# Modulation products two at a time inside the attentions of a two-layer diffusion step

## Chip, cores and metric

One core of a Trainium2 chip runs the whole program. The metric is the device time of one execution in microseconds (us); less is better.

## The reference

Two trunk layers over 384 tokens: 128 context tokens and 256 latent tokens, D = 1024. What matters here, for each layer `l`:

```
sh1, sc1, g1, sh2, sc2, g2 = split(silu(c) @ w_ada[l] + b_ada[l], 6)   # adaLN, c and c_ctx; w_ada[l] is 1024 x 6144
h  = rmsnorm(x, norm1_g[l]) * (1 + sc1) + sh1
qa, ka, va, ub, qc, kc, vc = split(h @ w_in[l])
oA = differential attention(qa, ka, va)       # 4 heads, two maps each: softmax 0 - lam * softmax 1
oB = multi-scale pooling(ub)
oC = windowed attention(qc, kc, vc, sink)     # 8 heads, keys within 128, a sink
x  = x + g1 * (sum_n sigmoid(h @ w_gate[n]) * (o_n @ w_branch[n])) @ w_out[l]
h2 = rmsnorm(x, norm2_g[l]) * (1 + sc2) + sh2
x  = x + g2 * channel_mixer(h2)               # SwiGLU in layer 0, top-2-of-8 experts in layer 1
```

All inputs are float32. The new keys and values of the context tokens are outputs too.

## The kernel before

Tokens lie in three blocks of 128. Every engine has its own instruction order, written out by hand, and the engines meet at semaphores. Big weight matrices come through a ring of three slots in SBUF (`raw`, 1 MB each, two DMAs of 512 KB from SyncE's queue, function `halves`, L498). Most slots are split into a high part (`whi`, ScalarE) and a low part (`wlo`, VectorE), and multiplied in three passes (L734 to L736).

**The modulation products.** `w_ada` of a layer is 24 slots of 256 columns. A product (`ada_product`, L751) is eight small matmuls, 128 rows by 32 columns each, of the conditioning vectors against one raw slot of float32; it needs no split. All the products of one phase add into PSUM bank 7. Its last matmul raises `mm_done`, and SyncE starts the load of the slot three further on in the order only when that semaphore says that this slot's user is done. Phases 2 to 5 are the four attentions (layer 0: differential, windowed; layer 1: the same), with 8, 7, 6 and 6 products. The first two of each (numbers 0 and 1) run together before step 0; the others stand in the steps that `ADA_STEPS` (L80) names. Behind the products of a phase come, in the same ring, the two gate slots and the branch slot of the projection after the attention.

**An attention** (`attention`, kind 0 differential, kind 1 windowed) has twelve steps t: four heads or head pairs by three blocks of queries. Where t is a multiple of three the queries are context tokens with 128 keys, otherwise there are 384 keys. In step t TensorE runs, in this order,

- `scores(t + 2)`, for t from 2 to 9 (L977); it waits for the exponentials of step t, whose banks it reuses
- the modulation products of this step
- `transposes(t)` of the weights (L995); it waits for VectorE's `normal(t)`
- `values(t - 1)` (L1011); it waits for ScalarE's copy of the transposed weights

ScalarE runs in step t `exps(t + 1)` (L1662), which waits for VectorE's maxima of t + 1 and for `transposes(t - 1)`, and then the copy of the transposed weights (`pt_copy`, L1673). VectorE runs, for t from 3 on, `maxima(t)` (L2153; in kind 1 with a mask before it, L2151) and then `normal(t - 1)` (L2161 to L2164, or L2166 to L2168). In kind 0 it also copies a head's output after step 5, 8 and 11 (L2183), and in kind 1 it adds up a branch merge after `normal(4)` (`merge_sum`, L2208, which is queued ahead of `maxima(6)`). Near the end ScalarE splits the first gate slot in two halves (`gate_hi`, L1498). After step 11 TensorE goes on with the gate projection (L1068 and after).

S, P, T and V stand below for the scores, product, transposes and values of a numbered step or product: T9 is `transposes(9)`, P4 the product with i = 4. M is maxima, E exponentials, N `normal`.

Of the kernel before, what the change touches and what calls it, by code (L numbers as in the profile page):

```python
# [76 lines left out]
EARLY_BUF = {0: 0, 1: 1, 2: 2, 3: 3, 4: 4, 5: 0, 7: 1, 9: 2}  # L77
EARLY = 5
GROUPS = ADA_SLOTS[0] // 2
ADA_STEPS = {2: (1, 3, 5, 7, 9, 10), 3: (1, 4, 6, 8, 10), 4: (1, 4, 6, 9), 5: (1, 4, 6, 9)}  # L80
assert all(2 + len(ADA_STEPS[p]) == ADA_SLOTS[p] <= 16 for p in ADA_STEPS)
SQS = (0, 1, 1 + N_HALF, 2 + N_HALF)
SQ0 = (0, BLK, BLK + 5 * N_HALF, BLK + 5 + 5 * N_HALF)
# [56 lines left out]
def prefix_step_kernel(nc, a, outs, const):  # L140
    y_prompt, y_sample, new_dk, new_dv, new_wk, new_wv = outs
    ctx = ExitStack()
    with ctx:
# [239 lines left out]
        def ada_slot(phase, i):  # L383

            if phase == 0:
                return FIRST_ADA[i]
            if phase == 1:
                return ADA_SLOTS[0] + 3 + RING * i
            l, kind = (phase - 2) // 2, (phase - 2) % 2
            return gate_slot(l, kind + 1, 0, 0) - ADA_SLOTS[phase] + i  # L390
# [17 lines left out]
        def ada_raw(n):  # L408

            return early[:, EARLY_BUF[n], :] if n in EARLY_BUF else raw[:, n % RING, :]  # L410
# [43 lines left out]
        def weight_col(t):  # L454

            return 1 + (T - P if t % 3 == 0 and t else 0)
# [20 lines left out]
        def raw_wait(eng, n, more=0):  # L477
            if n in EARLY_BUF:
                eng.wait_ge(side_in[EARLY_BUF[n]], early_wait(n))
            else:  # L480
                eng.wait_ge(raw_in[n % RING], more + 32 * raw_turn(n))
# [249 lines left out]
        def _(pe):  # L731
# [10 lines left out]
            def ada_product(phase, i):  # L742

                n, last, bank = ada_slot(phase, i), ADA_SLOTS[phase] - 1, 7
                if phase == 0:
                    i, last = i % 2, 1
                raw_wait(pe, n)
                w = ada_raw(n).rearrange("p (k c) -> p k c", k=KD)
                for k in range(KD):
                    j = k % 4  # L750
                    mm = pe.matmul(ps[32 * j:32 * j + 32, bank, 0:256], sil32[:, k, 30 - 2 * i:62 - 2 * i], w[:, k, :],  # L751
                                   start=(i == 0 and k < 4), stop=(i == last and k >= 4), tile_position=(0, 32 * j))
                mm.then_inc(mm_done, 1)
# [17 lines left out]
            def ada_end(phase, g=0):  # L771
                n = 2 * (GAP_SLOTS[phase] if phase in GAP_SLOTS else ADA_SLOTS[phase]) if phase else 4
                pe.wait_ge(ada_row, ada_turn(phase) if phase else g + 1)
                for c in range(2):
                    mm = pe.matmul(ps[:, 7, 256 + 32 * c:256 + 32 * c + n], adarow[:, c * P:(c + 1) * P], pick[:, 0:n],
                                   start=True, stop=True)
                mm.then_inc(ada_turned, 1)
# [188 lines left out]
            def scores(l, kind, t):  # L966

                h, qb = t // 3, t % 3
                if t >= 2:
                    pe.wait_ge(e_done, 24 * l + 12 * kind + t - 1)  # L970
                nk, k0 = (P, 0) if qb == 0 else (T, P)
                q, kk = (qTA, kTA[:, h, k0:k0 + nk]) if kind == 0 else (qTC, kTC[:, h // 2, k0:k0 + nk])
                for m in range(2):
                    r = slice(64 * m, 64 * m + 64)
                    c0 = score_col(t) if kind else 0
                    out, lhs = ps[:, 2 * (t % 2) + m, c0:c0 + nk], q[r, h, qb * P:(qb + 1) * P]
                    mm = pe.matmul(out, lhs, kk[r], start=True, stop=True)  # L977
                mm.then_inc(s_done, 1)

            def attention(l, kind):  # L980

                st0 = 24 * l + 12 * kind
                it0 = 24 * l + 12 * kind
                phase = 2 + 2 * l + kind

                def transposes(t):
                    pe.wait_ge(p_done, st0 + t + 1)
                    if kind:
                        pe.wait_ge(pt_evac, it0 + t)
                    elif it0 + t >= 2:  # L990
                        pe.wait_ge(pt_evac, it0 + max(t - 1, 0))
                    k0 = kind * weight_col(t)
                    for m in range(1 + kind):
                        for kb in range(1 if t % 3 == 0 else 3):
                            mm = pe.transpose(ps[:, 4 + (m if kind else t % 2), kb * P:(kb + 1) * P],  # L995
                                              ebuf[:, t % 2, m, k0 + kb * P:k0 + (kb + 1) * P], ident)
                    mm.then_inc(tp_done, 1)

                def values(t):
                    h, qb = t // 3, t % 3  # L1000
                    pe.wait_ge(pt_evac, it0 + t + 1)
                    grp = 8 * l + 4 * kind + h
                    if qb == 0 and grp >= 1:
                        pe.wait_ge(o_evac, grp)
                    c = slice(h * P, (h + 1) * P) if kind == 0 else slice(512 + (h // 2) * 64, 576 + (h // 2) * 64)
                    keys = [vtok[:, 0, c]] if qb == 0 else [vtok[:, 1, c], vtok[:, 2, c], ctxv[:, c]]
                    for kb, v in enumerate(keys):
                        k = slice(kb * P, (kb + 1) * P)
                        for m in range(1 + kind):
                            rows, x = (slice(64 * m, 64 * m + 64), ptm[:, t % 2, m, k]) if kind else (slice(0, P), pt[:, t % 2, k])  # L1010
                            mm = pe.matmul(ps[rows, 6, qb * P:(qb + 1) * P], v, x, start=(kb == 0),  # L1011
                                           stop=(kb == len(keys) - 1))
                    mm.then_inc(pv_done, 1)

                scores(l, kind, 2)
                scores(l, kind, 3)
                pe.wait_ge(merge_top, 2 * l + kind + 1)
                ada_product(phase, 0)
                ada_product(phase, 1)
                if kind == 0:  # L1020
                    pe.wait_ge(merge_done, 6 * l + 2)
                else:
                    pe.wait_ge(merge_read, 4 * l + 2)
                for t in range(12):
                    if t >= 2 and t + 2 < 12:
                        scores(l, kind, t + 2)
                    if t in ADA_STEPS[phase]:
                        ada_product(phase, 2 + ADA_STEPS[phase].index(t))
                    transposes(t)
                    if t >= 1:  # L1030
                        values(t - 1)
                    if t == 11 and kind == 1:
                        ada_end(phase)
                values(11)
# [422 lines left out]
            for l in range(DEPTH):  # L1457
                if l:
                    mean_squares(2 * l)
                input_projection(l)  # L1460
                branch(l, 0)
                attention(l, 0)
                branch(l, 1)
                attention(l, 1)
                branch(l, 2)
                out_projection(l)
                mean_squares(2 * l + 1)
                if l == 0:
                    units()
                else:  # L1470
                    router()
                    experts()
# [1196 lines left out]
```

## Time and profile before

| | |
|---|---|
| median of three runs | 1483.82 us (1482.88 to 1486.86) |
| profiled execution, own time | 1485.04 us |
| its span, first to last instruction | 1482.8 us |
| TensorE busy | 1454.4 us, 98% of the span |
| VectorE, ScalarE busy | 901.8 us (61%), 734.1 us (50%) |
| mean granted share of TensorE's clock | 0.996 |

The span is what the trace shows; the own time has 2.24 us around it. The four attentions begin with their products 0 and 1 at 194.83, 276.27, 844.07 and 924.18 us, and the next gate projection starts at 220.56, 307.29, 868.48 and 954.33 us.

### The profile page before, as it was taken

The page shows a single profiled execution, that of the slowest core. Times are in us where ns is not written, and L with a number is a line of the kernel's source. Part 1 is how long each engine was busy: PE and PEld are TensorE (multiplying, and loading weights), DVE is VectorE, ACT ScalarE, POOL GpSimd, SP SyncE. Part 2 cuts the span into 40 slices and gives each one's busy share as a digit, 9 for nine tenths or more (in the row PEclk, how much of TensorE's full clock was granted, in tenths as well). Part 3 has the DMA queues.
Part 4 walks back from the last instruction along what each step waited for, and adds up shares of the span by engine and source line. Part 5 has one row for each costly group of instructions (what it writes and reads, how often), then busy time and mean ns, then how long its engine had stood idle before and what let it go on. Part 6 is the DMA issues. An engine that isn't in the chain of part 4 may idle for free.

```text
span 1482.8 us, 22302 instructions
## 1 busy us (share of the span) xinstructions
PE 1454.4 (98%) x8911; PEld 1277.9 (86%) x8911; DVE 901.8 (61%) x1077; ACT 734.1 (50%) x872; POOL 49.4 (3%) x53
## 2 busy tenths in 40 slices
PE   7999999999999999999999999999899999999998
PEld 5788969789999999998889879699788888888884
DVE  4543265555654245336532373736799999999886
ACT  4433354453442242225434272733678787787753
POOL 0100000000000000001000000000000000000020
PEclk9999999999999999999999999999999999999999
DMA  9854365468763445364432371646499999999991
GB/s 328 285 174 150 114 222 176 137 203 272 240 186 102 129 125 142 114 213 145 152 125 91 102 234 59 225 144 206 141 378 385 383 390 389 383 383 388 350 336 50
DMA packets 228137, 324.36 MB, mean 219 GB/s; under 512 B 8373, under 2 KB 154718, under 8 KB 227790
## 3 DMA queue, kind: packets, MB, share of 16 engines
q1 hardware_dynamic: 219728, 296.02, 58.8%
q0 software_dynamic: 6256, 23.77, 4.4%
q10 hardware_dynamic: 2062, 3.24, 0.6%
q8 instruction: 71, 1.16, 0.3%
q14 instruction: 20, 0.16, 0.0%
HBM read 308.05 MB, written 14.95 MB: 218 GB/s over the span
## 4 chain that ended last, share of the span: by engine, by line
PE 93%; DVE 3%; SPq 2%; ACT 1%; DMA 1%; issue 1%; ACTq 0%; DVEq 0%
PE ps L734 26%; PE ps L736 26%; PE ps L735 26%; PE ps L751 2%; PE ps L977 2%; PE ps L1011 1%; PE ps L995 1%; SPq L498 1%; PE ps L1233 1%; PE ps L1273 1%; DMA early<-in_w_ada_dram 1%; PE ps L832 1%; PE ps L761 0%; PE ps L956 0%; ACT ebuf L1662 0%
## 5 line engine op out<-in xcount | busy, mean ns | idle before, releaser
L734 PE MATMUL ps<-hhi,whi 128*128 128x384 f32 x824 | 276.6, 336 | 0.3 <-DVE hidlo L2554 0.3
L736 PE MATMUL ps<-hhi,wlo 128*128 128x384 f32 x824 | 275.4, 334 | 0.0
L735 PE MATMUL ps<-hlo,whi 128*128 128x384 f32 x824 | 275.3, 334 | 0.0
L1980 DVE TENSOR_TENSOR wlo<-raw,whi 128x2048 fp32r<-128x2048 f32 x64 | 146.4, 2289 | 176.5 <-ACT whi L1488 164.6
L734 PEld LDWEIGHTS ps<-hhi,whi 128*128 128x128 f32 x824 | 154.7, 188 | 2.4 <-issue 2.0
L735 PEld LDWEIGHTS ps<-hlo,whi 128*128 128x128 f32 x824 | 154.7, 188 | 0.3
L736 PEld LDWEIGHTS ps<-hhi,wlo 128*128 128x128 f32 x824 | 154.6, 188 | 0.0
L2440 DVE TENSOR_TENSOR wlo<-mraw,whi 128x2048 fp32r<-128x2048 f32 (+2 forms) x72 | 143.5, 1992 | 15.0 <-ACT whi L1759 14.6
L1759 ACT ACTIVATE whi<-mraw 128x2048 fp32r<-128x2048 f32 (+2 forms) x72 | 120.9, 1679 | 58.5 <-PE ps L736 57.4
L1488 ACT ACTIVATE whi<-raw 128x2048 fp32r<-128x2048 f32 x60 | 114.5, 1911 | 70.4 <-PE ps L736 58.8
L2440 DVE TENSOR_TENSOR wlo<-raw,whi 128x2048 fp32r<-128x2048 f32 (+2 forms) x72 | 144.2, 2018 | 8.1 <-ACT whi L1759 7.7
L734 PE MATMUL ps<-whi,xgh 128*128 128x512 f32 (+1 forms) x384 | 145.9, 380 | 0.2 <-DVE xgl L2429 0.2
L736 PE MATMUL ps<-whi,xgl 128*128 128x512 f32 (+1 forms) x384 | 142.7, 372 | 0.0
L735 PE MATMUL ps<-wlo,xgh 128*128 128x512 f32 (+1 forms) x384 | 142.7, 372 | 0.0
L1759 ACT ACTIVATE whi<-raw 128x2048 fp32r<-128x2048 f32 (+2 forms) x72 | 121.6, 1698 | 30.9 <-PE ps L736 30.7
L734 PE MATMUL ps<-whi,hhi 128*128 128x512 f32 (+1 forms) x285 | 108.6, 381 | 2.8 <-issue 2.0
L2540 DVE TENSOR_TENSOR wlo<-raw,whi 128x2048 fp32r<-128x2048 f32 (+1 forms) x36 | 76.1, 2113 | 57.9 <-ACT whi L1736 57.9
L736 PE MATMUL ps<-whi,hlo 128*128 128x512 f32 (+1 forms) x285 | 106.1, 372 | 0.0
L735 PE MATMUL ps<-wlo,hhi 128*128 128x512 f32 (+1 forms) x285 | 105.9, 372 | 0.0
L1736 ACT ACTIVATE whi<-raw 128x2048 fp32r<-128x2048 f32 (+1 forms) x36 | 63.8, 1771 | 54.4 <-PE ps L736 54.4
L734 PEld LDWEIGHTS ps<-whi,xgh 128*128 128x128 f32 x384 | 72.1, 188 | 12.2 <-issue 2.0
L736 PEld LDWEIGHTS ps<-whi,xgl 128*128 128x128 f32 x384 | 72.1, 188 | 10.2
(397 smaller groups left out, 2495.0 us busy)
## 6 DMA issues: line engine op xcount, KB each, us to landing
raw<-in_w_ada_dram SPq DMA_DIRECT2D x62, 512.0 KB, 5.2
raw<-in_w_gate_dram SPq DMA_DIRECT2D x48, 512.0 KB, 4.6
raw<-in_w_ex_up_dram SPq DMA_DIRECT2D x24, 1024.0 KB, 7.8
raw<-in_w_ex_down_dram SPq DMA_DIRECT2D x24, 1024.0 KB, 7.8
raw<-in_w_in_dram SPq DMA_DIRECT2D x43, 512.0 KB, 6.1
raw<-in_w_ex_gate_dram SPq DMA_DIRECT2D x16, 1024.0 KB
mraw<-in_w_ex_gate_dram SPq DMA_DIRECT2D x16, 1024.0 KB, 8.4
mraw<-in_w_ex_down_dram SPq DMA_DIRECT2D x16, 1024.0 KB, 8.6
```

Of the source, the lines that this page charges most:

```text
L498: sp.dma_start(dst[i], src[i]).then_inc(side_in[EARLY_BUF[n]] if n in EARLY_BUF else raw_in[n % RING], 16)
L734: pe.matmul(out, s[0], m[0], start=first, stop=False, **kw)
L735: pe.matmul(out, s[0], m[1], start=False, stop=False, **kw)
L736: return pe.matmul(out, s[1], m[0], start=False, stop=last, **kw)
L751: mm = pe.matmul(ps[32 * j:32 * j + 32, bank, 0:256], sil32[:, k, 30 - 2 * i:62 - 2 * i], w[:, k, :], start=(i == 0 and k < 4), stop=(i == ...
L977: mm = pe.matmul(out, lhs, kk[r], start=True, stop=True)
L1488: act.activation(whi[:, n % RING, :], raw[:, n % RING, :], copy).then_inc(hi_done, 1)
L1736: act.activation(whi[:, s % RING, 0:used], raw[:, s % RING, 0:used], copy).then_inc(hi_done, 1)
L1759: act.activation(whi[:, m % RING, c:E_USED[m]], mraw[m % MRAW][:, c:E_USED[m]], copy).then_inc(hi_done, 1)
L1980: dve.tensor_tensor(wlo[:, n % RING, :], raw[:, n % RING, :], whi[:, n % RING, :].bitcast(F32), ALU.subtract).then_inc(lo_done, 1)
L2440: dve.tensor_tensor(wlo[:, m % RING, c:E_USED[m]], mraw[m % MRAW][:, c:E_USED[m]], whi[:, m % RING, c:E_USED[m]].bitcast(F32), ALU.subtrac ...
L2540: dve.tensor_tensor(wlo[:, s % RING, 0:used], raw[:, s % RING, 0:used], whi[:, s % RING, 0:used].bitcast(F32), ALU.subtract).then_inc(lo_d ...
```

## The change

The same products run in the same order, with the same weights and into the same bank. Only the steps in which they stand are others: where one product stood in each of four to six steps, two now stand in each of two or three steps (the second attention keeps a single one in step 10). In the loop the single test becomes a loop over all products of the step.

```diff
--- before.py
+++ after.py
@@ -77,7 +77,7 @@
 EARLY_BUF = {0: 0, 1: 1, 2: 2, 3: 3, 4: 4, 5: 0, 7: 1, 9: 2}
 EARLY = 5
 GROUPS = ADA_SLOTS[0] // 2
-ADA_STEPS = {2: (1, 3, 5, 7, 9, 10), 3: (1, 4, 6, 8, 10), 4: (1, 4, 6, 9), 5: (1, 4, 6, 9)}
+ADA_STEPS = {2: (3, 3, 6, 6, 9, 9), 3: (3, 3, 7, 7, 10), 4: (4, 4, 9, 9), 5: (4, 4, 9, 9)}
 assert all(2 + len(ADA_STEPS[p]) == ADA_SLOTS[p] <= 16 for p in ADA_STEPS)
 SQS = (0, 1, 1 + N_HALF, 2 + N_HALF)
 SQ0 = (0, BLK, BLK + 5 * N_HALF, BLK + 5 + 5 * N_HALF)
@@ -1024,8 +1024,9 @@
                 for t in range(12):
                     if t >= 2 and t + 2 < 12:
                         scores(l, kind, t + 2)
-                    if t in ADA_STEPS[phase]:
-                        ada_product(phase, 2 + ADA_STEPS[phase].index(t))
+                    for i, step in enumerate(ADA_STEPS[phase]):
+                        if step == t:
+                            ada_product(phase, 2 + i)
                     transposes(t)
                     if t >= 1:
                         values(t - 1)
```

`ADA_STEPS[phase][i]` is the step of product i + 2. The first attention goes from P2 to P7 in steps 1, 3, 5, 7, 9, 10 to 3, 3, 6, 6, 9, 9; the second from P2 to P6 in 1, 4, 6, 8, 10 to 3, 3, 7, 7, 10; the third and fourth from P2 to P5 in 1, 4, 6, 9 to 4, 4, 9, 9.

## Rows read from the trace of the kernel before

**Rows 1.** The page's busy time, share of the span and instructions of each engine:

```profile
PE 1454.4 (98%) x8911; PEld 1277.9 (86%) x8911; DVE 901.8 (61%) x1077; ACT 734.1 (50%) x872; POOL 49.4 (3%) x53
```

**Rows 2.** The page's chain that ended last, shares of the span by engine:

```profile
PE 93%; DVE 3%; SPq 2%; ACT 1%; DMA 1%; issue 1%; ACTq 0%; DVEq 0%
```

**Rows 3.** Stretches (us): busy PE, PEld, DVE, ACT, POOL (instructions), clock, DMA share, GB/s:

```profile
197.00:221.00 24.00, 23.48 (x215) 14.89 (x215) 16.71 (x43) 17.20 (x55) 0.00 (x0) 1.00 1.00 321
276.00:308.00 32.00, 30.49 (x326) 18.57 (x323) 21.14 (x51) 21.72 (x59) 0.00 (x0) 1.00 0.73 231
843.00:869.00 26.00, 25.02 (x224) 15.93 (x224) 19.81 (x47) 17.43 (x55) 0.00 (x0) 1.00 0.77 243
924.00:955.00 31.00, 29.42 (x308) 18.02 (x307) 21.87 (x51) 21.99 (x61) 0.00 (x0) 1.00 0.63 204
```

**Rows 4.** TensorE's timeline, first attention's opening: start, us, what [idle before]:

```profile
194.83 1.93 PE L751 MATMUL ps<-raw,sil 128*32 128x256 f32 x32
196.69 0.33 PE L995 MATMUL ps<-cst,ebuf 128*128 128x128 f32 x1
196.95 1.07 PE L751 MATMUL ps<-raw,sil 128*32 128x256 f32 x16
197.95 0.55 PE L995 MATMUL ps<-cst,ebuf 128*128 128x128 f32 x3
...
198.65 0.92 PE L977 MATMUL ps<-kTA,qTA 64*128 64x384 f32 x4
199.62 0.55 PE L995 MATMUL ps<-cst,ebuf 128*128 128x128 f32 x3
```

**Rows 5.** VectorE's timeline there: the weights of step 2 finished:

```profile
198.94 0.62 DVE L2164 SCALAR_TENSOR_TENSOR ebuf<-ebuf,small 128x384 f32<-128x384 f32 x1
```

**Rows 6.** TensorE's timeline, first attention's closing:

```profile
215.49 0.33 PE L995 MATMUL ps<-cst,ebuf 128*128 128x128 f32 x1
...
218.42 0.55 PE L995 MATMUL ps<-cst,ebuf 128*128 128x128 f32 x3 [0.23 <-DVE ebuf L2164]
...
219.87 0.71 PE L1011 MATMUL ps<-pt,vtok 128*128 128x128 f32 x4 [0.24 <-ACT pt L1673]
```

**Rows 7.** Timeline of all engines, from scores of step 8 to weights of step 7:

```profile
207.74 0.92 PE L977 MATMUL ps<-kTA,qTA 64*128 64x384 f32 x4
...
208.70 0.96 DVE L2153 TENSOR_REDUCE small<-ps 128x2 f32<-128x768 f32 x1 [1.32 <-PE ps L977]
...
209.51 0.49 PE L977 MATMUL ps<-kTA,qTA 64*128 64x128 f32 x4
...
210.02 0.62 DVE L2164 SCALAR_TENSOR_TENSOR ebuf<-ebuf,small 128x384 f32<-128x384 f32 x1
```

**Rows 8.** TensorE's timeline, second attention:

```profile
281.53 0.88 PE L995 MATMUL ps<-cst,ebuf 128*128 128x128 f32 x6
...
289.31 0.87 PE L995 MATMUL ps<-cst,ebuf 128*128 128x128 f32 x6 [0.62 <-DVE ebuf L2168]
...
290.91 0.92 PE L977 MATMUL ps<-kTC,qTC 64*128 64x384 f32 x4
```

**Rows 9.** VectorE's timeline, second attention:

```profile
280.69 0.42 DVE L2168 TENSOR_SCALAR ebuf<-ebuf,small 128x384 f32<-128x384 f32 x1
...
286.31 1.75 DVE L2208 TENSOR_TENSOR macc<-macc,gbuf 128x1536 f32<-128x1536 f32 x1
...
293.75 0.41 DVE L2168 TENSOR_SCALAR ebuf<-ebuf,small 128x384 f32<-128x384 f32 x1
```

**Rows 10.** First attention's loads issued at 198.4 and at 202.7 us: time to landing:

```profile
DMA to landing us min/median/max: 7.6/8.2/8.7
...
DMA to landing us min/median/max: 6.3/6.9/7.4
```

**Rows 11.** The stretch with the lower clock, columns as in Rows 3:

```profile
678.40:685.20 6.80, 6.80 (x45) 4.61 (x48) 1.56 (x5) 0.26 (x1) 0.00 (x0) 0.50 0.48 157
```

**Rows 12.** TensorE's timeline there, a product between other stages:

```profile
680.49 1.93 PE L761 MATMUL ps<-gap,sil 128*32 128x256 f32 x16
```

## The prediction

> **What bounds the kernel now.** I read the page's busy times and its chain of waits first. TensorE is busy 98% of the span and holds 93% of the chain [rows 1, 2]: a microsecond that is added to or taken from its own queue arrives at the end, unless a wait takes it up. Then the busy time by stretch: in the four attentions TensorE is still busy for 23.5 of 24.0, 30.5 of 32.0, 25.0 of 26.0 and 29.4 of 31.0 us, 4.6 us of idling in all, while VectorE and ScalarE work 66 to 76% of each [rows 3]. So these stretches are TensorE's work with a few small waits, and the question is which waits the products now cover. The timelines say that step by step.
>
> **What a product costs.** Alone it takes 1.00 us from its start to the next instruction (196.95 to 197.95). The pair ahead of step 0 takes 1.86 (194.83 to 196.69) [rows 4]. So the second of a pair costs 0.86, and each pair saves 0.14 against two single ones. The change makes 3 + 2 + 2 + 2 = 9 new pairs: 9 x 0.14 = 1.26 us less work. It adds no instruction and no DMA.
>
> The Trainium skill (TensorEngine Tiling (Array Packing), Key Properties) has a rule for this: changing the tiling mode, not just the tile, drains the engine. By that rule each pair makes two mode changes fewer; the pair in the trace agrees in sign, and the page gives no time.
>
> **What limits TensorE when no product stands in a step.** Three chains, read from starts and ends.
> - Kind 0, middle: S8 starts at 207.74, M8 at 208.70, and N7, behind it on VectorE, ends at 210.02 + 0.62 = 210.64 [rows 7]. So T(t+1) can't start before S(t+2) + 2.95 (0.05 for the semaphore). TensorE's own work between them is S8 with T6 and V5 (207.74 to 209.51, 1.77 [rows 7]) and S9, of one block of keys (0.43, its 0.49 less the overlap). With a product among them there is no wait; without one T7 must wait.
> - Kind 1, the same with the mask: S8 starts at 290.91 [rows 8], N7 ends at 293.75 + 0.41 = 294.16 [rows 9]: S + 3.30.
> - Both ends of an attention. Opening: E2 waits for T0, and N2 ends at 198.94 + 0.62 = 199.56 [rows 5], which is when T2 starts (199.62) [rows 4]. Closing in kind 0: E11 follows T9 on ScalarE and N11 follows E11, so T11 starts 218.42 - 215.49 = 2.93 after T9 [rows 6] whatever TensorE does between.
>
> **First attention.** P2 leaves step 1. There it was covered: without it, V0 and S4 wait for ScalarE and T2 starts at 199.62 as before. In step 3, beside P3, it costs its 0.86. P4 and P5 go from steps 5 and 7 together into step 6: -0.14, and by the chain counts about 0.06 of wait each in T5 and T8, +0.12. P7 leaves step 10, where it stood inside the fixed 2.93 between T9 and T11; in step 9, ahead of T9, it costs 0.86. Last, V11 waited until 219.87 [rows 6] for a ScalarE copy behind half a gate split; from T11 to the projection it was 220.56 - 218.42 = 2.14, and with that wait gone T11, V10 and V11 take about 1.8: -0.3 to -0.36. Sum 0.86 - 0.14 + 0.12 + 0.86 - 0.36 = **+1.3**.
>
> **Second attention.** T2 followed S4 at 281.53 without a wait [rows 8], while N2 had ended at 280.69 + 0.42 = 281.11 [rows 9]: taking P2 out of step 1 gives back 0.37, no more. P2 and P3 in step 3 cost 1.86 and P3 leaves step 4 (-1.00), but T5 had a wait of 0.62 there [rows 8], for VectorE, behind `merge_sum` (286.31, 1.75 us [rows 9]), that swallows most of it. Counting E5 behind T3 and the output copy on ScalarE, T5 comes out 0.12 later than before. Then P4 leaves step 6 and P5 step 8 (-2.00, and a wait of 0.19 before S10 goes), and the pair in step 7 costs 1.86: -0.33. Sum **-0.2**. P6 stays in step 10.
>
> **Third attention.** P2 from covered step 1 into step 4: +0.86. P4 leaves step 6: -1.00, but S8 to T7 is then 1.77 + 0.43 = 2.20 of work against 2.95: T7 waits 0.75, and V6 and T8 wait 0.2 more behind it: +0.94. P4 in step 9 beside P5: +0.86. Sum **+1.66**.
>
> **Fourth attention.** T2 -0.37; P2 into step 4 +0.86; the wait before T5 (0.69 here) goes; P4 leaves step 6 -1.00; T7 waits 0.84 (S + 3.30 against 2.46 of work); two waits before S10 and T8 (0.32) go; P4 in step 9 +0.86. Sum -0.37 + 0.86 - 0.69 - 1.00 + 0.84 - 0.32 + 0.86 = **+0.2**.
>
> Together 1.33 - 0.20 + 1.66 + 0.18 = **+3.0 us**. The 1.26 saved is in it: without it the waits would add 4.2.
>
> **The loads.** A product also frees a slot. In the first attention the load of slot 5 starts after P2, at 202.75 where it was 198.4, and P5 wants it at 209.4, so 6.2 us are left for its second half. At 202.7 us a load with two others in flight took 6.3 to 7.4 us [rows 10]; now only one is in flight, its own 1 MB takes 3 us at the 321 GB/s of this stretch [rows 3], and it lands at about 207.6. I cost it at nothing; 1.8 us cover it. Slot 7 starts after P4 (209.5) for 216.2, with the same margin. In the third and fourth attention gate slot 1 now loads after P4 in step 9, some 6 us later; ScalarE splits it about 8 us after that issue, against landing times of 3.5 to 8.7. In the worst of these only ScalarE would wait, with 2.5 us before TensorE needs the slot. What follows an attention depends on it alone (the projections are relative to TensorE's progress), so I carry the sum to the end in full.
>
> The profiled execution's span of 1482.8 would become 1485.8 and its own time 1488.0. It lay 1.2 above the median; on the median 1483.82 + 3.0 = **1486.8 us**.
>
> **Rivals.**
> 1. *The loads decide; slower.* If slot 5 and slot 7 take the 8.7 us of the worst row [rows 10], P5 waits from 209.4 to 211.9 and P7 2.4 more; 3.0 + 4.9 gives 1491.7. For it: the memory queue is full in this stretch. Against: that row stood behind two other loads. It decides from landing times over 6.2 us. 10%.
> 2. *The pairing pays; not slower, or a little faster.* The waits are small and ScalarE and VectorE are a quarter to a third idle [rows 3]. If they catch up while TensorE is in a pair, only the 0.14 per pair is left: 1483.8 - 1.3 = 1482.6, -0.1%. Against: catching up is bounded, since S(t+2) must have run before VectorE can go ahead, and it is issued before the pair. It decides from T7 in the third attention: does it wait? 17%.
> 3. *The clock; slower.* In the attentions TensorE had its 2.4 GHz throughout, gaps of up to 0.7 us included (granted clock 1.00 [rows 3]). But it fell to 1.2 GHz for 6.8 us at 678.4 [rows 11], when the engine had just run the sums of squares, matmuls of a single column; a product took 1.93 there [rows 12] against 1.07 [rows 4]. Such a stretch costs up to 3.4 us. The change thins out TensorE's work in the opening and in steps 5 to 7, and it shifts all later stages by some us; if one more such stretch appears, 3.0 + 3.4 gives 1490.2. It decides from a granted clock under 1.00 in any of the four stretches, or a third dip elsewhere. 6%. The Trainium skill (TensorE: Matmul & The Clock Gate, Part 1) has the rule that activity holds the clock up and lack of it lets it drop; the trace agrees with that at 678 us, and shows it in no attention.
>
> **Numbers.** Forecast 64%, rival 2 17%, rival 1 10%, rival 3 6%, something else 3%. My counts could be wrong by 1.5 us in either direction, the difference between medians by about as much (the three runs spread over 4 us). About 0.3%, 4.5 us, is what a measurement of this kernel tells from no change, so the forecast and rival 2 both mean "no change" nearly always. Same 0.83, slower 0.15, faster 0.02. The range takes in rival 2 and reaches almost to rival 3, and leaves out rival 1: 1482.6 to 1490.
>
> **What the changed profile would show.** Pairs of 1.86 us everywhere. T2 at 199.6 in the first attention with about 0.8 us of waits before S4 and V0; T11 there with a wait near 1.0 instead of 0.23; T7 of the third and fourth attention waiting 0.75 and 0.84 for VectorE. The attentions, from product 0 to the gate projection, longer by 1.3, -0.2, 1.7 and 0.2 us (25.7, 31.0, 24.4 and 30.2 before). Idling in the four stretches about 4.2 us more. No product waiting for a load. The prediction is wrong if a product does wait for one, if T2 of the first attention moves with P2, or if the shift is not found again at the end of the span.

## The result, and the profile after

The changed kernel takes 1487.23 us in the median of 11 runs (1485.74 to 1489.99) against 1483.82 in 11 runs of the kernel before (1482.48 to 1487.17). The two medians are 3.4 us apart; the ratio over all runs is 1.0018, 95% interval 1.0010 to 1.0026: 2.7 us more, between 1.5 and 3.9. That is a loss that eleven runs can tell from nothing, and inside the 0.3% that counted as "no change". The forecast was 1486.8, +3.0.

The busy times of the page are those of before [rows 1] to within 0.2%. The instructions are the same, and so are their kinds:

```profile
span 1485.1 us, 22302 instructions
...
PE 1452.3 (98%) x8911; PEld 1277.8 (86%) x8911; DVE 902.1 (61%) x1077; ACT 733.2 (49%) x872; POOL 49.4 (3%) x53
```

The four attentions, each timed in the timeline from its product 0 to the first matmul of the gate projection behind it:

| attention | before | after | difference | predicted |
|---|---|---|---|---|
| first | 25.74 | 27.72 | +1.98 | +1.33 |
| second | 31.02 | 30.81 | -0.20 | -0.20 |
| third | 24.40 | 26.05 | +1.65 | +1.66 |
| fourth | 30.15 | 30.23 | +0.08 | +0.18 |
| sum | | | +3.51 | +2.97 |

The predicted values are from the sums of the prediction. The two stretches right behind a differential attention, up to the windowed one, are the same to 0.02 us in both traces (55.71 and 55.70 before, 55.71 and 55.69 after). The profiled spans differ by 2.3 us, not 3.5; where the other 1.2 went is told below.

TensorE's timeline of the changed kernel, first attention. To be read beside [rows 4] and [rows 6], 0.11 us earlier at its start:

```profile
194.72 1.93 PE L751 MATMUL ps<-raw,sil 128*32 128x256 f32 x32
...
198.40 0.92 PE L977 MATMUL ps<-kTA,qTA 64*128 64x384 f32 x4 [0.64 <-ACT ebuf L1663]
199.51 0.55 PE L995 MATMUL ps<-cst,ebuf 128*128 128x128 f32 x3 [0.19 <-DVE ebuf L2165]
...
201.50 1.94 PE L751 MATMUL ps<-raw,sil 128*32 128x256 f32 x32
203.37 0.33 PE L995 MATMUL ps<-cst,ebuf 128*128 128x128 f32 x1
...
208.34 1.93 PE L751 MATMUL ps<-raw,sil 128*32 128x256 f32 x32
210.20 0.33 PE L995 MATMUL ps<-cst,ebuf 128*128 128x128 f32 x1
...
215.31 1.07 PE L751 MATMUL ps<-raw,sil 128*32 128x256 f32 x16
216.69 1.07 PE L751 MATMUL ps<-raw,sil 128*32 128x256 f32 x16 [0.30 <-DMA raw<-in_w_ada_dram]
217.69 0.33 PE L995 MATMUL ps<-cst,ebuf 128*128 128x128 f32 x1
...
219.43 0.46 PE L1011 MATMUL ps<-pt,vtok 128*128 128x128 f32 x2 [0.42 <-DVE oraw L2184]
220.62 0.55 PE L995 MATMUL ps<-cst,ebuf 128*128 128x128 f32 x3 [0.73 <-DVE ebuf L2165]
```

The pairs take 1.87 us (201.50 to 203.37) and 1.86. T2 starts 4.79 us after product 0, in both kernels, now with waits of 0.64 before S4 and 0.19 before T2 in the place of the product of step 1. T11 waits 0.73 where it waited 0.23, and V9 0.42 before it. And one thing was not forecast: the second product in step 9 waits 0.30 for its load (216.69), so those two take 2.38. Two other kernels with the same steps from 6 on don't have that wait; more on it below.

The same view of the third and the fourth attention, where T7 waits for VectorE, 0.69 and 0.79 where 0.75 and 0.84 were forecast:

```profile
859.75 0.49 PE L977 MATMUL ps<-kTA,qTA 64*128 64x128 f32 x4
860.94 0.55 PE L995 MATMUL ps<-cst,ebuf 128*128 128x128 f32 x3 [0.69 <-DVE ebuf L2165]
```

```profile
943.47 0.49 PE L977 MATMUL ps<-kTC,qTC 64*128 64x128 f32 x4
944.76 0.87 PE L995 MATMUL ps<-cst,ebuf 128*128 128x128 f32 x6 [0.79 <-DVE ebuf L2169]
```

Busy time by stretch, columns as in [rows 3]. The first stretch had 0.5 us of idling before; it has 2.4 now, the third 2.2 where it had 1.0. Taken from product 0 to the gate projection, the four attentions idle for 8.7 us where they idled for 4.6, that is 4.1 more for the 4.2 of the prediction:

```profile
197.00:221.00 24.00, 21.61 (x199) 13.12 (x197) 16.64 (x42) 15.36 (x52) 0.00 (x0) 1.00 0.92 307
...
843.00:869.00 26.00, 23.81 (x213) 14.84 (x211) 19.06 (x46) 14.98 (x52) 0.00 (x0) 1.00 0.59 186
```

### The profile page after: what moved, and what is told of

Same layout as the page of the kernel before. It is cut to its first block, busy times and chain, and to the rows that moved or that the text cites. A ratio compares the mean times of both kernels' runs of the same rounds, so it can differ in the third digit from the quotient of the medians.

```text
span 1485.1 us, 22302 instructions
## 1 busy us (share of the span) xinstructions
PE 1452.3 (98%) x8911; PEld 1277.8 (86%) x8911; DVE 902.1 (61%) x1077; ACT 733.2 (49%) x872; POOL 49.4 (3%) x53
## 4 chain that ended last, share of the span: by engine, by line
PE 92%; DVE 3%; DMA 2%; ACT 1%; issue 1%; SPq 0%; DVEq 0%; ACTq 0%
PE ps L734 26%; PE ps L736 25%; PE ps L735 25%; PE ps L751 2%; PE ps L977 2%; PE ps L1011 1%; PE ps L995 1%; DMA mraw<-in_w_ex_up_dram 1%; PE ps L761 1%; DMA early<-in_w_ada_dram 1%; PE ps L832 1%; PE ps L1274 1%; DVE macc L2001 0%; PE ps L956 0%; DVE wlo L2441 0%
```

## The experiments

Two theories. **Cover**: a product costs nothing where TensorE would wait for the softmax chain anyway, 1.00 us alone or 0.86 behind another elsewhere, and the change moves products out of covered steps. **Pairs**: two at a time cost by themselves, by the burst that holds up ScalarE and VectorE or by the loads that start later. The table has what each kernel's own trace shows for the four attentions, as differences to the kernel before; the two rows of the thin kernels are read below. Each row is one traced execution. The changed kernel was also timed over eleven runs, by_waits and mixed over twelve each; of the others there is only the one time (1483.9 to 1491.3 us), and nothing is concluded from it.

| kernel | steps of the products | 1st | 2nd | 3rd | 4th |
|---|---|---|---|---|---|
| changed | 3,3,6,6,9,9 / 3,3,7,7,10 / 4,4,9,9 / 4,4,9,9 | +1.98 | -0.20 | +1.65 | +0.08 |
| thin_before | as before, four thin products | 0.00 | 0.00 | -0.07 | -0.45 |
| thin_after | as changed, the same four thin | +1.03 | -0.63 | +1.20 | -0.37 |
| open_back | 1,3,6,6,9,9 / 1,3,7,7,10 / 1,4,9,9 / 1,4,9,9 | +0.60 | -0.33 | +0.79 | +0.28 |
| late_back | 3,3,6,6,9,10 / 3,3,6,8,10 / 4,4,6,9 / 4,4,6,9 | +1.21 | +0.13 | +0.86 | -0.19 |
| pairs_covered | 1,3,5,7,10,10 / 1,4,4,7,10 / 1,4,10,10 / 1,4,10,10 | -0.10 | -1.03 | +0.11 | +0.10 |
| by_waits | 1,4,7,10,10,11 / 1,4,4,7,10 / 1,4,7,10 / 4,4,7,10 | +2.11 | -0.26 | -0.45 | -0.52 |
| loads_triple | 3,3,5,6,9,9 / 3,3,7,7,9 / 1,10,10,10 / 4,4,7,9 | +1.62 | -0.19 | +3.70 | -0.53 |
| halves | as before, each product cut in two | +1.29 | +0.44 | +1.09 | +0.33 |
| mixed | 1,3,5,7,10,10 / 1,4,4,7,10 / 1,4,7,10 / 4,4,7,10 | -0.14 | -0.59 | -0.45 | -0.53 |

All but the thin kernels and halves differ from the changed kernel only in the tuple `ADA_STEPS`.

### Thin products: the same work taken out of both kernels

Four products, one in each attention, keep only the last of their eight matmuls; what the other seven would have added is missing from the outputs. The edit, cut to its core:

```diff
-            def ada_product(phase, i):
+            def ada_product(phase, i, ks=range(KD)):
...
-                for k in range(KD):
+                for k in ks:
...
+                        thin = (phase, i) in ((2, 2), (3, 3), (4, 4), (5, 4))
+                        ada_product(phase, i, range(7, 8) if thin else range(KD))
```

> The kernel before, with four products cut to the last of their eight matmuls (so four column groups of the modulations are wrong by the parts left out): P2 (step 1) of the first attention, P3 (step 4) of the second, P4 (step 6) of the third, P4 (step 6) of the fourth. About 0.75 us of TensorE's work is gone in each. Cover theory (a product between the scores and the transposes of those steps stands where TensorE would wait anyway): the four attentions change by 0.0, 0.0, -0.06 and -0.5 us. Rival (TensorE's queue is the bound throughout, so products cost their time wherever they stand): -0.75 in each.

> The changed kernel with the same four products cut to their last matmul. Cover theory: here each of them stands on the path, so against the changed kernel the attentions shrink by 0.75, 0.5, 0.75 and 0.75 us (one that follows its pair's first may save 0.1 less). Rival (the change costs because of bursts or late loads, not by lost cover): the same savings as in the kernel before, whatever they are.

Measured, the saving is 0.00, 0.00, 0.07 and 0.45 us in the kernel before, and 0.96, 0.43, 0.45 and 0.45 in the changed one. TensorE's timeline of thin_before, first attention:

```profile
194.50 1.93 PE L751 MATMUL ps<-raw,sil 128*32 128x256 f32 x32
...
196.63 0.62 PE L751 MATMUL ps<-raw,sil 128*32 128x256 f32 x2
197.18 0.55 PE L996 MATMUL ps<-cst,ebuf 128*128 128x128 f32 x3
...
198.19 0.92 PE L978 MATMUL ps<-kTA,qTA 64*128 64x384 f32 x4 [0.24 <-ACT ebuf L1665]
199.30 0.55 PE L996 MATMUL ps<-cst,ebuf 128*128 128x128 f32 x3 [0.19 <-DVE ebuf L2167]
```

One matmul of the eight still takes 0.55 us to the next instruction (196.63 to 197.18), where the product took 1.00. So 0.45 us is what was really taken out, not 0.75: my size was off. That 0.45 goes into waits in the first attention (0.24 before S4, 0.19 before T2), and T2 starts 4.80 us after product 0, as before. In the first three attentions the product was covered. In the fourth it was covered in part: T7 now waits 0.24 for VectorE, but the waits behind it (0.19 before S10, 0.14 before T8) are gone, and the sum is 0.45 again. In the changed kernel every one of the four gives its whole 0.45 back. The first gives 0.96, since P7 waits for no load in this kernel: its last pair takes 1.87 (214.77 to 216.64). The thin product doesn't explain that, as both the load of P7's slot and P7 itself come 0.45 sooner. The cover theory holds in seven of the eight values as told, with 0.45 in the place of 0.75, and in the eighth with the load added. Queue-bound throughout is refuted: three of four products cost nothing before.

### Opening and closing put back, one at a time

> The changed kernel with the first of the moved products back in step 1: steps 1,3,6,6,9,9 / 1,3,7,7,10 / 1,4,9,9 / 1,4,9,9. Cover theory, against the kernel before: +0.5, -0.3, +0.8, +0.4 us (the changed kernel has +2.0, -0.2, +1.65, +0.1). In the third attention half of the loss goes, since T2 starts when VectorE lets it; in the fourth it gets worse by 0.3, since there step 1 is covered only in part and the product in step 4 was covered by the wait behind the merge sum. Rival (bursts): each loses in proportion to its pairs, so the first attention keeps two thirds, the third and fourth one half.

> The changed kernel with its later pairs undone in part: steps 3,3,6,6,9,10 / 3,3,6,8,10 / 4,4,6,9 / 4,4,6,9. Cover theory, against the kernel before: +0.8, +0.1, +0.9, -0.2 us. In the first attention the whole of the last pair's cost is gone, the wait of the last product for its load as well. Rival (the late load is what the change costs in the first attention): only the 0.3 to 0.5 us of that wait comes back there, so it stays at +1.5 or more.

open_back came out as counted: +0.60, -0.33, +0.79 and +0.28 were measured for +0.5, -0.3, +0.8 and +0.4. Its last pair of the first attention, in step 9 like that of the changed kernel, takes 1.86 and waits for no load. The rival's proportional shares would be about +1.3, +0.8 and 0 in the first, third and fourth. The third can't tell the two apart; the first and the fourth go with cover. late_back came out as counted in three attentions and at +1.21 instead of +0.8 in the first. There the last product is back in step 10 and waits for no load. ScalarE's timeline shows what is late in its place:

```profile
219.06 0.49 ACT L1674 ACTIVATE pt<-ps 128x384 f32<-128x384 f32 x1 [0.74 <-PE ps L995]
219.71 1.06 ACT L1499 ACTIVATE whi<-raw 128x1024 fp32r<-128x1024 f32 x1 [0.16 <-DMA raw<-in_w_gate_dram]
220.67 0.47 ACT L1674 ACTIVATE pt<-ps 128x384 f32<-128x384 f32 x1
```

The split of the first gate slot waits 0.16 for its load, the copy of T11's weights is queued behind it, and V11 waits 0.51 for that copy where it waited 0.24 before [rows 6]. SyncE had needed 1.58 us to issue the half ahead of it, slot 7's second, against a median of 0.51. The first row is that issue, the second, from a view of the next microsecond, how long the two gate halves then took:

```profile
L498 SPq DMA_DIRECT2D raw<-in_w_ada_dram x1: 1577/1577/1577, 210.1 to 210.1; - x1
```

```profile
L498 SPq DMA_DIRECT2D raw<-in_w_gate_dram x2: 508/630/751, 211.7 to 212.3; - x2
...
DMA to landing us min/median/max: 6.3/6.8/7.4
```

So the gate slot was issued at 211.7, where it was 211.1 before and 210.4 in the changed kernel. That the slow issue alone made it late is not shown: in the changed kernel its second half was issued 1.1 us sooner after product 0 (at 211.0), took 8.5 us and landed as far behind product 0. Of the 0.4 above the forecast 0.3 is V11's longer wait. The other 0.1 stands before T8, which comes 0.95 us later than in the kernel before, in this kernel as in the changed one; +0.84 was counted. The late-load rival named the wrong load and expected +1.5 or more; it fails too.

### Pairs where TensorE waits, and products by the waits

> Pairs, but only in steps where the chains leave TensorE waiting: steps 1,3,5,7,10,10 / 1,4,4,7,10 / 1,4,10,10 / 1,4,10,10. Cover theory: against the kernel before -0.1, -1.0, +0.2, 0.0 us, so a pair costs nothing by itself. Rival (two products at a time are what costs): a loss of 0.5 to 1 us per pair in each attention.

Measured -0.10, -1.03, +0.11, +0.10: a pair costs nothing by itself. The second attention, with a pair in step 4 behind `merge_sum`'s wait, is a full microsecond shorter.

> Products put where TensorE waits: steps 1,4,7,10,10,11 / 1,4,4,7,10 / 1,4,7,10 / 4,4,7,10. Cover theory: against the kernel before -0.8, -1.0, -0.4, -0.6 us, together -2.9, so about 0.2% faster (ratio 0.998). Rival (pairs cost by themselves, or the waits come back elsewhere, at the gate projection or in the loads): no gain, or a loss like that of the changed kernel in the attentions that have a pair (first, second, fourth).

Ratio 1.0014 (1.0004 to 1.0024): slower. This one missed. The third and fourth attention give what was told (-0.45, -0.52), the second -0.26 in place of -1.0, the first +2.11 in place of -0.8, and the stretch behind it another 1.58. In the second, with the same steps as in pairs_covered, P4 waited for its load and the pair took 0.77 longer:

```profile
291.03 1.07 PE L751 MATMUL ps<-raw,sil 128*32 128x256 f32 x16 [0.56 <-DMA raw<-in_w_ada_dram]
```

ScalarE and TensorE in the first:

```profile
216.91 0.49 ACT L1674 ACTIVATE pt<-ps 128x384 f32<-128x384 f32 x1 [1.03 <-PE ps L995]
220.62 1.06 ACT L1499 ACTIVATE whi<-raw 128x1024 fp32r<-128x1024 f32 x1 [3.22 <-DMA raw<-in_w_gate_dram]
221.59 0.47 ACT L1674 ACTIVATE pt<-ps 128x384 f32<-128x384 f32 x1
```

```profile
222.11 0.71 PE L1011 MATMUL ps<-pt,vtok 128*128 128x128 f32 x4 [2.87 <-ACT pt L1674]
```

With P5 in step 10 the first gate slot's load starts after step 10, and ScalarE waits 3.22 us for it, with the copy for V11 queued behind. My count for this kernel had the products' own loads in it and left out the gate slot's. TensorE then stands still for 2.87 us, and the clock goes:

```profile
223.30:226.70 3.40, 3.40 (x14) 3.40 (x12) 2.03 (x1) 1.92 (x3) 0.00 (x0) 0.51 0.85 309
```

For 3.4 us the granted clock is 0.51, and matmuls of the gate projection that take 0.34 take 0.52. The stretch up to the windowed attention, 55.7 us in every other trace, takes 57.29 here. The four attentions make +0.88 and this 1.58: 2.5 us together, and the ratio says 2.1 (0.6 to 3.6).

### An earlier load, and three in a row

> Steps 3,3,5,6,9,9 / 3,3,7,7,9 / 1,10,10,10 / 4,4,7,9. First attention: P4 alone in step 5, so the slot of P7 is loaded some 2 us earlier than in the changed kernel: if P7's wait there was for its load, it is gone and the last pair takes 1.86 us instead of 2.38; the attention comes to +1.4 against the kernel before (changed kernel +2.0). If the wait stays, it was not the load. Third attention: three in a row in step 10: 1.00 + 0.86 + 0.86 = 2.72 us if each product after the first saves 0.14; 2.86 if only one of them does; the attention +1.0. Second -0.1, fourth -0.5.

```profile
206.49 1.07 PE L751 MATMUL ps<-raw,sil 128*32 128x256 f32 x16
207.49 0.55 PE L995 MATMUL ps<-cst,ebuf 128*128 128x128 f32 x3
...
215.60 1.93 PE L751 MATMUL ps<-raw,sil 128*32 128x256 f32 x32
217.47 0.33 PE L995 MATMUL ps<-cst,ebuf 128*128 128x128 f32 x1
```

With P4 in step 5 the last pair takes 1.87 us, as was told for a wait that is the load's. It proves less than it was meant to, because open_back and thin_after lose the wait too, without an earlier P4. The attention stands at +1.62 against +1.98; +1.4 was told.

```profile
864.00 2.80 PE L751 MATMUL ps<-raw,sil 128*32 128x256 f32 x48
866.73 0.55 PE L995 MATMUL ps<-cst,ebuf 128*128 128x128 f32 x3
...
871.69 0.81 PE L1011 MATMUL ps<-pt,vtok 128*128 128x128 f32 x4 [2.90 <-ACT pt L1674]
```

Three in a row take 2.73 us: each product behind another saves 0.14. The third attention as a whole missed, +3.70 for +1.0, in the same way as by_waits: P3 in step 10 holds back the first gate slot (TensorE waits 2.90 before V11), and 3.4 us at half the clock follow (57.05 for 55.70 behind it).

### What the 0.14 us are

In the loop, with `ks` as in the thin kernels and `mm_done` raised by the second half alone:

```diff
                     if t in ADA_STEPS[phase]:
-                        ada_product(phase, 2 + ADA_STEPS[phase].index(t))
+                        ada_product(phase, 2 + ADA_STEPS[phase].index(t), range(4))
                     transposes(t)
+                    if t in ADA_STEPS[phase]:
+                        ada_product(phase, 2 + ADA_STEPS[phase].index(t), range(4, KD))
```

> The kernel before with each product inside the steps cut in two halves of four matmuls, one before the transposes and one after them; no work is left out, but TensorE changes between kinds of matmul twice more per product. If the 0.14 us that a pair saves is the price of such a visit, each half takes about 0.57 us to the next instruction (0.43 + 0.14), a product 1.14 in all. The attentions grow by 0.3, 0.4, 0.3, 0.2 us where this is not covered. Rival (the 0.14 is no price of changing kinds but a start-up of the first product of a step, such as waiting for its slot's semaphore): the second half takes 0.43.

```profile
196.85 0.64 PE L751 MATMUL ps<-raw,sil 128*32 128x256 f32 x8
197.42 0.55 PE L996 MATMUL ps<-cst,ebuf 128*128 128x128 f32 x3
197.90 0.64 PE L751 MATMUL ps<-raw,sil 128*32 128x256 f32 x8
198.47 0.49 PE L1012 MATMUL ps<-pt,vtok 128*128 128x128 f32 x2
198.88 0.92 PE L978 MATMUL ps<-kTA,qTA 64*128 64x384 f32 x4
```

Each half takes 0.57 us (196.85 to 197.42, 197.90 to 198.47), 0.43 + 0.14, the second as much as the first. So 0.14 is a price of each visit and no start-up of the step; the rival fails. The sizes of the attentions missed: +1.29, +0.44, +1.09, +0.33 for +0.3, +0.4, +0.3, +0.2. The neighbours pay too: T1 takes 0.48 to the next start, where it takes 0.39 ahead of V0 [rows 4: 197.95, with V0 at 198.34], and V0 takes 0.41, where it took 0.31. That is 0.2 more per product than I counted: the added visit, between transposes and values, costs some 0.33 in all.

### The placement that the runs point to

> Steps 1,3,5,7,10,10 / 1,4,4,7,10 / 1,4,7,10 / 4,4,7,10: each attention has the placement that came out best so far without holding back a gate slot's load. Theory (a product costs nothing where TensorE waits, 0.86 to 1.00 us elsewhere, provided that no load of a later slot comes late by it): the attentions take -0.1, -1.0, -0.45, -0.5 us against the kernel before, together -2.1 us or a ratio of 0.9986, and ScalarE's first half of the first gate slot waits for no load. Rival (the gain of the second attention seen in one run, and of the fourth in two, does not survive as time of the whole, because it is given back between the attentions): ratio 1.000.

Ratio 0.9989, 95% interval 0.9980 to 0.9997: 1482.98 us in the median of 12 runs against 1485.17 of 17 runs of the kernel before on the same chip. It beats the kernel before by 0.11%, and, by the two ratios, the changed one by about 0.3%; the two were not run side by side. The attentions took -0.14, -0.59, -0.45 and -0.53, together -1.71, and the ratio gives -1.6 (-3.0 to -0.4). ScalarE's split of the first gate slot waits for no load in the first and third attention. In the second, P4 in step 4 waited for its load:

```profile
285.38 1.07 PE L751 MATMUL ps<-raw,sil 128*32 128x256 f32 x16
286.68 1.07 PE L751 MATMUL ps<-raw,sil 128*32 128x256 f32 x16 [0.23 <-DMA raw<-in_w_ada_dram]
287.68 0.88 PE L995 MATMUL ps<-cst,ebuf 128*128 128x128 f32 x6
```

so 0.44 of the microsecond that pairs_covered had gained there is missing, though the two kernels have the same steps in this attention. The wait parts the pair too: it takes 2.30 (285.38 to 287.68). In pairs_covered it takes 1.87:

```profile
285.60 1.93 PE L751 MATMUL ps<-raw,sil 128*32 128x256 f32 x32
```

In by_waits, the third kernel with these steps, it took 2.63. What differs is the landing of slot 4's second half: 10.0 us after product 0 in pairs_covered, 10.6 here and 10.9 in by_waits, with P4 ready for it at 10.3. When it was issued doesn't order them: 3.5, 3.9 and 3.4 us after product 0. Here SyncE had taken 1.73 us over the issue of slot 3's second half, and in pairs_covered 1.35 over that of slot 4's first. So the margin is 0.3 us, and the load's own time varies by more than that, with steps that are the same. The 62 issues of halves of `w_ada` in the trace of before take 0.37 to 1.79 us, at a median of 0.51, from one and the same line of code. Why one sometimes takes three times as long stays open, and so does why the landing times spread.

## Why the prediction was right

**The time and its sign.** Forecast +3.0, measured +2.7 (1.5 to 3.9). The likeliest case came in, not a rival: pairs save 0.14 each, and the waits uncovered cost more. That the number came so close is in part luck. In the profiled execution the attentions took 3.51 us more, 0.5 of it by a load that was forecast to cost nothing, and the rest of the execution gave 1.2 back. Of the three signs of being wrong that the prediction names, T2 did not move with P2. A product did wait for a load, in the profiled execution. And the shift is found at the end of the span only as 2.3 us.

**What a product costs.** Right: 1.00 alone, 0.86 behind another, also for the third of three. The count of 9 pairs held but for one, which the load split. The Trainium skill's rule that a change of tiling mode drains the engine (TensorEngine Tiling (Array Packing), Key Properties) fits what halves shows, two visits at the same price; that the 0.14 us are a drain is argued, not shown. The prediction's "two mode changes fewer" for each pair is too many where scores stand ahead, which is so in steps 2 to 9. The rows have scores as `64*128` and transposes as `128*128`, so the kind of matmul changes there with or without a product. In halves the visits between transposes and values, both `128*128`, are the ones for which the neighbours pay 0.2 more.

**What limits TensorE.** Right in all three chains: T2 4.79 us after product 0 in both kernels; T11 2.93 us after T9 before, 220.62 - 217.69 = 2.93 after; T7 2.96 us after S8 in the third attention (857.98 to 860.94) for 2.95, and 3.30 in the fourth (941.46 to 944.76). The thin products show the other half, that work in those places was free before.

**Attention by attention.** Second, third and fourth within 0.1 us. The first took +1.98 for +1.33, and 0.52 of the difference is the pair with P7: in this execution the loads' 0 was too little. I gave slot 7 what its own 1 MB takes once the queue is free. It was issued at 209.5 and 209.9, as foreseen, and its halves took 4.5 us and more:

```profile
L498 SPq DMA_DIRECT2D raw<-in_w_ada_dram x2: 367/438/508, 209.5 to 209.9; - x2
...
DMA to landing us min/median/max: 4.5/5.6/6.8
```

The second half took the 6.8 us and landed 0.05 us before P7 starts at 216.69. thin_after and open_back have the same steps from 6 on, and there P7's slot is issued just as long before the last pair (5.8 us), with the gate slot's load behind it as well, its first half half a microsecond later, its second at 1.7 us and not 1.1. Its halves take 4.1 and 5.1 us, and 4.2 and 5.2, and P7 waits for nothing. thin_after:

```profile
DMA to landing us min/median/max: 4.1/4.6/5.1
```

So the load behind alone did not make it late. What differs more is the load ahead, slot 6, whose second half was issued at 204.2 in the changed kernel and at 203.6 in thin_after. It took 9.6 us, until 213.8, well into slot 7's time, and 6.9 us, until 210.5:

```profile
DMA to landing us min/median/max: 9.6/9.6/9.6
```

```profile
DMA to landing us min/median/max: 6.9/6.9/6.9
```

That this pushed slot 7 back is argued, and why it took 9.6 us stays open. P7 waited 0.30, the pair took 0.52 longer, and with T9 later by that it all went to the end. Without it the first attention comes to +1.46, and open_back (+0.60, and 0.86 for its product in step 1) and thin_after (+1.03, and 0.45) give 1.46 and 1.48. So the placement leaves P7 a margin that one of three such traces used up, and the forecast's 0 holds in the other two. Slot 5's landing, the one that the prediction worried about most, was in time. Rival 1 was thus right in kind for one product in one execution, and in size for a tenth (0.5 of 4.9). The remaining 0.13 is small waits: before T8 they are 0.21 (0.07 at S10, 0.14 at T8) where 0.12 was counted for T5 and T8, and the end of the attention gives back 0.33 and not 0.36.

**The carry to the end.** I carried the sum in full. Up to the next attention that is right to 0.02 us. Over the long stretches it can't be read from one execution: the second to third attention took 536.32 us for 536.78, the end 527.84 for 528.49. The granted clock may be part of it. Before, it fell to 0.50 for 3.4 us behind the last out projection; after, it didn't there:

```profile
1040.20:1043.60 3.40, 3.40 (x18) 3.40 (x18) 0.41 (x2) 1.29 (x2) 0.00 (x0) 0.50 0.00 0
```

```profile
1042.00:1046.00 4.00, 3.84 (x35) 3.76 (x35) 1.32 (x3) 1.78 (x4) 0.00 (x0) 1.00 0.06 23
```

Of the eleven traces of this study, all eleven have such a dip near 680 us; six have one near 395, and six, not the same, one near 1040. They come and go between kernels that are identical there. The 4 to 5 us that runs of one kernel spread over fit with that, but no run here separates it.

**Rival 3** (the clock falls in an attention) did not come in for this change, whose longest wait is 0.79 us. It did in by_waits and loads_triple, where TensorE stood still for 2.9 us. The Trainium skill's rule (TensorE: Matmul & The Clock Gate, Part 1) that lack of activity lets the clock drop agrees with both. It agrees less well with the dip near 680 us of the kernel before: TensorE ran matmuls of one column ahead of that one, and the profile counts it busy for all of the 2 us before. I had priced such a stretch at up to 3.4 us; 3.4 us at half the clock cost 1.58 and 1.35.

**Rival 2** (the waits stay away) is refuted by T7 of the third and fourth attention, which wait 0.69 and 0.79.

## What to carry to other kernels

On an engine that is 98% busy, small work that fits in anywhere is free where that engine waits, so list its waits step by step and put the work between the instruction that starts a chain and the one that waits for it; merging two pieces saves one visit (0.14 us here) and can uncover a wait of five times that. Then follow what each piece frees: here a product late by some steps delayed the load of the slot three further on, and behind that load ScalarE held a copy that TensorE needed. Two placements that counted only the chains lost 2.9 and 2.7 us against their forecast in an attention by it, and 1.6 and 1.4 behind it. The mixed one that kept the early loads early gained 1.6 us (0.4 to 3.0) over the kernel before. Look at more than one trace before you call a small wait for a load the placement's: with the same steps the loads of one pair cost 0, 0.4 and 0.8 us.

## What was not expected of the hardware

One matmul of 128 rows by 32 columns over 256 columns takes TensorE 0.55 us to the next instruction, four of them, one in each column group, 0.57, and eight 1.00, the change included. So the four groups run side by side, 0.43 us per round, and seven eighths of a product's matmuls are 45% of its time.

The time of a 1 MB load varies with steps that are the same. Its halves took 3.5 and 4.5 us to land with nothing issued beside them (before, 297.7 and 298.1). With the next load issued half a microsecond behind they took 4.1 and 5.1, 4.2 and 5.2, and, with the load ahead still landing, 4.5 and 6.8 (slot 7 in thin_after, open_back and the changed kernel). And the time that SyncE needs to issue one such half goes from 0.37 to 1.8 us between issues by the same line of code.
